# A decoder layer on eight cores: residual adds moved to GpSimd, norm steps spread over the blocks, w_ada pieces moved from the down to the up groups

## The reference

```python
mod = silu(c) @ w_ada + b_ada                       # (B, 6D), D = 2048
shift_m, scale_m, gate_m, shift_f, scale_f, gate_f = split(mod, 6)
h = rms_norm(x, g_pre_mix) * (1 + scale_m) + shift_m
u, v, p, ga, gb = split(h @ w_in)                   # 9216 columns
y_a = spatial_gating(gelu(u), gelu(v), ...) @ w_branch_a
y_b = multiscale_pool(p, ...) @ w_branch_b
mix = (sigmoid(ga) * y_a + sigmoid(gb) * y_b) @ w_out
x = x + gate_m * rms_norm(mix, g_post_mix)
h = rms_norm(x, g_pre_ffn) * (1 + scale_f) + shift_f
up = causal_depthwise_conv(h @ w_up, conv_w, conv_b) # 2 * 5632 columns
a, g = split(up, 2)
x = x + gate_f * rms_norm((gelu(a) * g) @ w_down, g_post_ffn)
```

## Time and profile before

| | us |
|---|---|
| median of 3 runs | 2220.53 |
| lowest, highest | 2217.82, 2484.43 |
| the profiled execution | 2215.26 |
| its span on the slowest core (core 2) | 2213.3 |
| spans of the eight cores | 2198.2 to 2213.3 |
| TensorE matmul busy | 1886.2 (85%) |
| VectorE, ScalarE, GpSimd busy | 714.1, 550.8, 67.2 |

### The profile page before, as it was taken

How to read it: one execution, slowest core, us unless ns; L and a number is a source line. 1 busy time by engine, 2 the same in 40 slices (tenths; PEclk the granted TensorE clock), 3 DMA queues, 4 the chain that set the end, 5 groups by cost and what they waited for, 6 DMA issues and landing times.

```text
span 2213.3 us, 28189 instructions; the slowest of 8 cores (2198.2 to 2213.3 us)
## 1 busy us (share of the span) xinstructions
PE 1886.2 (85%) x12028; PEld 1125.5 (51%) x12028; DVE 714.1 (32%) x832; ACT 550.8 (25%) x722; POOL 67.2 (3%) x113
## 2 busy tenths in 40 slices
PE   0325996999999999999876898799989999899995
PEld 0102443646646565665543564356634665366554
DVE  0114005340111112332556453123532354224535
ACT  0304114100002211113445532024310432034321
POOL 0000000000000000000000000000000000000002
PEclk9857998969999999999998999899999999999998
DMA  9596654642676357555392434553344333443409
GB/s 189 142 168 122 112 93 84 110 81 39 115 133 112 61 96 129 109 106 127 102 175 83 72 72 81 99 101 72 65 91 93 77 67 68 95 85 68 90 16 152
DMA packets 36380, 218.70 MB, mean 99 GB/s; under 512 B 2849, under 2 KB 19489, under 8 KB 24097
## 3 DMA queue, kind: packets, MB, share of 16 engines
q0 software_dynamic: 20192, 187.71, 47.8%
q1 hardware_dynamic: 16066, 29.21, 4.2%
HBM read 379.43 MB, written 16.78 MB: 179 GB/s over the span
## 4 chain that ended last, share of the span: by engine, by line
PE 76%; DMA 7%; DVE 5%; ACT 5%; SPq 3%; issue 3%; DVEq 0%; ACTq 0%; POOLq 0%; POOL 0%
PE ps L289 57%; PE ps L439 6%; PE ps L780 3%; PE ps L1021 3%; PE ps L568 3%; DMA RING<-w_ada 2%; SPq L328 2%; DMA RING<-w_down 2%; SPq L683 1%; DMA RC<-xT 1%; PE ps L494 1%; DMA R<-xT 1%; DMA RING<-w_in 1%; PE ps L488 1%; ACT SC L454 1%
## 5 line engine op out<-in xcount | busy, mean ns | idle before, releaser
L289 PE MATMUL ps<-RD,RING 128*128 128x342 bf16 (+1 forms) x3360 | 578.0, 333 | 73.5 <-DMA RING<-w_down 46.0
L289 PE MATMUL ps<-RC,RING 128*128 128x342 bf16 x3696 | 539.2, 308 | 7.1 <-ACT R L901 7.1
L289 PEld LDWEIGHTS ps<-RD,RING 128*128 128x128 bf16 x3360 | 328.1, 98 | 319.4 <-issue 87.4
L289 PEld LDWEIGHTS ps<-RC,RING 128*128 128x128 bf16 x3696 | 358.6, 97 | 187.6 <-issue 7.4
L842 DVE SCALAR_TENSOR_TENSOR SC<-SC,vec 128x1024 f32<-128x1024 f32 x77 | 98.9, 1285 | 284.7 <-ACT SC L840 284.7
L925 ACT ACTIVATE SC<-ps 128x1026 f32<-128x1026 f32 x77 | 79.0, 1027 | 408.5 <-PE ps L289 399.4
L289 PE MATMUL ps<-R,RING 128*128 128x342 bf16 x1152 | 172.0, 310 | 0.9 <-DVE R L503 0.9
L439 PE MATMUL ps<-RING,RD 128*128 128x512 bf16 x576 | 127.2, 384 | 25.0 <-ACT RD L404 25.0
L289 PEld LDWEIGHTS ps<-R,RING 128*128 128x128 bf16 x1152 | 112.0, 98 | 59.5 <-issue 2.5
L439 PEld LDWEIGHTS ps<-RING,RD 128*128 128x128 bf16 x576 | 56.7, 99 | 94.6 <-issue 28.8
L844 DVE SCALAR_TENSOR_TENSOR SC<-SC,vec 128x1024 f32<-128x1024 f32 x77 | 98.9, 1284 | 8.4 <-DVE SC L842 0.5
(11 more groups left out here) (131 smaller groups left out, 1278.1 us busy)
## 6 DMA issues: line engine op xcount, KB each, us to landing
RING<-w_ada POOLq DMA_DIRECT2D x24, 2048.0 KB, 27.5
RING<-w_in POOLq DMA_DIRECT2D x18, 2048.0 KB, 16.9
RING<-w_up POOLq DMA_DIRECT2D x16, 2048.0 KB, 13.1
RING<-w_down POOLq DMA_DIRECT2D x12, 1408.0 KB, 11.0
RING<-w_up POOLq DMA_DIRECT2D x8, 1536.0 KB, 10.5
R<-xT SPq DMA_DIRECT2D x15, 576.0 KB, 43.6
R<-xT SPq DMA_DIRECT2D x6, 1368.0 KB, 24.3
RING<-w_branch_a POOLq DMA_DIRECT2D x4, 2048.0 KB, 15.8
```

Source lines behind the costliest of these rows:

```text
L289: e.matmul(o, lhsT=l, rhs=r, start=st, stop=sp),
```

## The change

Seven edits:

1. Weight loads get `max_dma_last_dim=4096`: a contiguous run is cut into pieces of at most 4096 bytes of the float32 source (2048 bytes of bf16).
2. The residual parts come from a second input `xP`, laid out on the host so that a partition's 8 channel blocks are one run of 10944 bytes, instead of 8 runs of 1368.
3. The residual add goes from VectorE to GpSimd.
4. The inverse norms of the mix chain lie in PSUM banks 4 and 5, not in SBUF. The mix projection and pass C then take their banks in turn from 0 to 3, pass AB pairs 0/1 and 2/3.
5. The chain of a part is 17 entries of `later` instead of 10: root, invert, 8 pairs, drain, drain and second root, second invert, 4 norms of 4 channel blocks. The ones matmuls follow two pairs later. The last block of a part runs two entries.
6. Mod pieces 20 to 23 move from the down groups behind the first up piece of (group 0, half 1), (1, 0), (1, 1), (2, 0).
7. In the last down group the reciprocal is a queue entry of its own, one entry after an empty one, instead of following the sqrt at once.

```diff
+    xP = din("xP", [3, 128, 16 * 342])
...
-            tok = P.dma("pool", lambda e: e.dma_start(out=flat, in_=src), sem, deps=deps)
+            tok = P.dma("pool", lambda e: e.dma_start(out=flat, in_=src, max_dma_last_dim=4096), sem, deps=deps)
...
-        rstd_m, rstd_x = sc_bufs(12 * 171, PN, 2, F32)
-        tf = sc_bufs(12 * 171 + 2 * PN, PN, 4, F32)
+        tf = sc_bufs(12 * 171, PN, 4, F32)
+
+        rstd_m, rstd_x = bank(4)[:, 0:PN], bank(5)[:, 0:PN]
...
+        def alloc_mid():
+            b = mid_next[0] % 4
+            mid_next[0] += 1
+            return b, bank_free[b]
...
         def load_x(t):
             for q in range(2):
-                P.dma("sp", lambda e, q=q: e.dma_start(out=x_buf[:, q * 8:(q + 1) * 8, :],
-                                                       in_=xT[q * 1024:(q + 1) * 1024, 126 + t * PN:126 + (t + 1) * PN].rearrange("(k p) n -> p k n", p=128)),
+                P.dma("sp", lambda e, q=q: e.dma_start(out=x_buf[:, q * 8:(q + 1) * 8, :].rearrange("p k n -> p (k n)"),
+                                                       in_=xP[t, :, q * 8 * PN:(q + 1) * 8 * PN]),
                       "xp%d" % t, deps=x_free)
...
-        def mix_chain(t, m, t_stat):
-
-            t_s, t_r = inv_rms(rstd_m, bank(6)[:, 0:PN], [t_stat, t_ggm] + rstd_m_free)
-            bank_free[6] = [t_s]
+        def mix_chain(t, m, get_stat):
...
+            def root():
+                state["s"] = P.op("act", lambda e: e.activation(out=rstd_m, in_=bank(6)[:, 0:PN], func=AF.Sqrt, bias=epst[:], scale=1.0),
+                                  deps=[get_stat(), t_ggm] + rstd_m_free)
+                bank_free[6] = [state["s"]]
+
+            def invert():
+                state["r"] = P.op("dve", lambda e: e.reciprocal(out=rstd_m, in_=rstd_m), deps=[state["s"]])
...
             def chunk(b):
                 t_a = P.op("dve", lambda e: e.scalar_tensor_tensor(out=m[:, b, :], in0=m[:, b, :], scalar=ggm[:, b:b + 1], in1=rstd_m,
-                                                                   op0=ALU.mult, op1=ALU.mult), deps=[t_r])
-                t_x = P.op("dve", lambda e: e.tensor_tensor(out=m[:, b, :], in0=m[:, b, :], in1=x_buf[:, b, :], op=ALU.add), deps=[t_a, x_tok[t]])
+                                                                   op0=ALU.mult, op1=ALU.mult), deps=[state["r"]])
+                rstd_m_free[:] = [t_a]
+                t_x = P.op("pool", lambda e: e.tensor_tensor(out=m[:, b, :], in0=m[:, b, :], in1=x_buf[:, b, :], op=ALU.add), deps=[t_a, x_tok[t]])
...
-                return stat2(b, t_sq)
+                pending.append(stat2(b, t_sq))
...
-            def finish():
-                t_s2, t_r2 = inv_rms(rstd_x, bank(7)[:, 0:PN], [state["tok"], t_gsf] + rstd_x_free)
...
             def pair(b):
                 def go():
-                    gos = [chunk(b), chunk(b + 1)]
+                    chunk(b)
+                    chunk(b + 1)
                     if b % 4 == 2:
                         spill_tok[t] = spill(b // 4)
                     if b == KC - 2:
                         x_free[:] = [xm_tok[-1]]
                         if t < 2:
                             load_x(t + 1)
-                    pending.append(gos)
+
+                    while len(pending) > 4:
+                        pending.pop(0)()
                 return go
...
+            def drain():
+                for g in pending[:2]:
+                    g()
+                del pending[:2]
...
+            def invert2():
+                state["r2"] = P.op("dve", lambda e: e.reciprocal(out=rstd_x, in_=rstd_x), deps=[state["s2"]])
+
+            def norm(b0):
                 def go():
...
+                    for b in range(b0, b0 + 4):
...
-            for b in range(0, KC + 2, 2):
-                later.append(step(b))
+            later.extend([root, invert] + [pair(b) for b in range(0, KC, 2)] + [drain, lambda: (drain(), root2()), invert2] + [norm(b) for b in range(0, KC, 4)])
...
-                b, bdeps = alloc_tm()
+                b, bdeps = alloc_mid()
...
-                run_later(1)
+                run_later(2 if blk == KC - 1 else 1)
...
-                def start_chain(t=t, m=m, last_stat=last_stat):
-                    mix_chain(t, m, last_stat())
-                later.append(start_chain)
+                mix_chain(t, m, prev)
...
-            i, bdeps = alloc_blk()
+            b0 = 2 * (m % 2)
+            bdeps = bank_free[b0] + bank_free[b0 + 1]
...
-            bk, bdeps = alloc_tm()
+            bk, bdeps = alloc_mid()
...
                     free_slot(s, tok)
+                    if mod_queue and p == 0:
+                        mod_piece(mod_queue.pop(0))
...
                     free_slot(s, tok)
-                    if mod_queue and (q == 0 or (k == 0 and q == 2)):
-                        mod_piece(mod_queue.pop(0))
...
         def finish_part(j, c0, n, t_stat):
-            t_s, t_r = inv_rms(rstd_y[j][:, 0:n], bank(6 + j % 2)[:, 0:n], [t_stat, t_ggf] + up_done)
+            t_s = P.op("act", lambda e: e.activation(out=rstd_y[j][:, 0:n], in_=bank(6 + j % 2)[:, 0:n], func=AF.Sqrt, bias=epst[:], scale=1.0),
+                       deps=[t_stat, t_ggf] + up_done)
             bank_free[6 + j % 2] = [t_s]
+            t_r = []
+
+            def invert():
+                t_r.append(P.op("dve", lambda e: e.reciprocal(out=rstd_y[j][:, 0:n], in_=rstd_y[j][:, 0:n]), deps=[t_s]))
...
+            fin_q.append(lambda: None)
+            fin_q.append(invert)
...
+        m["xP"] = np.ascontiguousarray(m["xT"][:, 126:].reshape(16, 128, 3, 342).transpose(2, 1, 0, 3).reshape(3, 128, 16 * 342))
```

More of the change, by code:

```diff
@@ L662, in build_program @@
         tf_free = [[] for _ in tf]
-        rstd_m_free = list(gates_done)
-        rstd_x_free = list(gates_done)
+        rstd_m_free = gates_done + bank_free[4]
+        rstd_x_free = gates_done + bank_free[5]
+        mid_next = [0]
+        def alloc_mid():
+            b = mid_next[0] % 4
+            mid_next[0] += 1
+            return b, bank_free[b]
         mix_buf = [part_f32[0], part_f32[2], part_f32[0]]
@@ L743, in go @@
                             load_x(t + 1)
-                    pending.append(gos)
-                return go
-            pending = []
-            def step(b):
-                def go():
-                    if b < KC:
-                        pair(b)()
-                    if len(pending) > (1 if b < KC else 0):
-                        for g in pending.pop(0):
-                            g()
-                    if b >= KC and not pending:
-                        finish()
-                return go
@@ new lines, in invert2 @@
+            def invert2():
+                state["r2"] = P.op("dve", lambda e: e.reciprocal(out=rstd_x, in_=rstd_x), deps=[state["s2"]])
+            def norm(b0):
+                def go():
+                    for b in range(b0, b0 + 4):
+                        f = b % 4
+                        t_a = P.op("dve", lambda e, b=b, f=f: e.scalar_tensor_tensor(out=tf[f], in0=m[:, b, :], scalar=gsf[:, b:b + 1], in1=rstd_x,
+                                                                                     op0=ALU.mult, op1=ALU.mult), deps=[state["r2"]] + tf_free[f])
+                        t_h = P.op("act", lambda e, b=b, f=f: e.activation(out=h2T[:, t, b, :], in_=tf[f], func=AF.Identity,
+                                                                           bias=mod_fm[:, 48 + b:49 + b], scale=1.0), deps=[t_a, mod_tok[15], part_pe[t]])
+                        tf_free[f] = [t_h]
+                        rstd_x_free[:] = [t_a]
+                    if b0 == KC - 4:
+                        if t == 0:
+                            t_h = P.op("dve", lambda e: e.tensor_scalar(out=h2T[:, 0, :, 0:2], in0=h2T[:, 0, :, 0:2], scalar1=hmask[:, 0:1], scalar2=None, op0=ALU.mult),
+                                       deps=[t_h, ldc_all])
+                        h2_tok[t] = t_h
+                        part_free[0 if t != 1 else 2] = [t_a, spill_tok[t]]
+                return go
@@ L805, in build_program @@
             if t < 2:
-                last_stat = prev
-                def start_chain(t=t, m=m, last_stat=last_stat):
-                    mix_chain(t, m, last_stat())
-                later.append(start_chain)
+                mix_chain(t, m, prev)
         mix_dead = tok
-        last_stat = prev
-        def start_chain_c():
-            mix_chain(2, mix_buf[2], last_stat())
-        later.append(start_chain_c)
+        mix_chain(2, mix_buf[2], prev)
         def ffn_up_specs(k, half):
@@ L873, in build_program @@
                     last = kc == KC - 1 and t == 1
-                    tok = P.op("pe", lambda e, i=i, t=t, kc=kc, wt=wt, bl=bl: e.matmul(bank(3 * i + t)[:, 0:PN], lhsT=wt[:, kc, bl * 128:(bl + 1) * 128],
+                    tok = P.op("pe", lambda e, b0=b0, t=t, kc=kc, wt=wt, bl=bl: e.matmul(bank(b0 + t)[:, 0:PN], lhsT=wt[:, kc, bl * 128:(bl + 1) * 128],
```

28 lines of the change are left out of this document (10 added, 18 removed).

## The result

The changed kernel takes 2142.05 us (median of three runs, 2139.89 to 2149.75) against 2220.53: a ratio of 0.966, with a 95% interval of 0.960 to 0.972. The forecast was 2127 us, with a range of its own of 2112 to 2135 and an outer one of 2103 to 2160. The time lies in the outer range and not in the inner. The gain is 78 us where 91 to 93 were expected.

A forecast was written before the change was run, and what follows sets the result against it. TensorE carries 76% of the span and its waits are what an edit can remove; the start is bound by DMA. Gains of 51.2 + 13.5 + 23 + 0 + 3 = 91 us gave 2127, range 2112 to 2135, outer 2103 to 2160.

The forecast's parts named there:

- Down groups: Down groups: without mod pieces the four w_down waits (46.0 us) and half-clock matmuls (4 x 1.3) go, gaining 51.2 us.
- The rest of C to last: Blocks behind pass C: the next needs the eighth L901, the second the eleventh; 1 us gained.
- AB and C: Passes AB and C: ScalarE's queue is the path, 8.9 us per block against 8.74 before; sum 0.
- Start: Kernel start: descriptors of 4096 bytes, queues taking turns one for one, release x at 60, not 73.5; 13.5 us gained.
- the second: Rival: x is not early (grouped packets or slow GpSimd), 9.5 to 13.5 us less gained, 2137 to 2141; chance 0.2.
- Mix blocks: Mix projection: a block takes 2.64 us, a part 42.2; the mix as a whole gains 23 us.
- The wait before AB: End of mix part 2: AB waits 5 us for ScalarE's last norm chunks plus 4 us for w_up.
- Part 0: First part of the mix projection: time as before, with no cost taken for finer load pieces.
- The add on GpSimd: Residual add: 1.0 us taken, between 0.52 and 2.29; in the mix it hides up to 1.3.
- Last group: Last down group: TensorE's waits of 2.94 and 0.96 us behind the reciprocals shrink to about 0.8; 3 us gained.
- multiply and add block each other: Part of rival 3 (chance 0.15): 3.14 us per block, +8 in the mix and +8 in AB, 2143.
- The fifth: Rival: cutting casting loads lowers their rate; at 200 GB/s 2325, deciding from about 225 down; chance 0.05.

The follow-up runs named there:

- e5: The kernel before with one edit only: w_ada (mod) pieces leave the down groups and follow the up pairs; 2170.1 us, ratio 0.9782.
- e2: The changed kernel with the three w_up loads of AB planned as their buffers come free, ahead of later adds on GpSimd's queue; 2138.8 us, ratio 0.9636.
- e4: The changed kernel with the residual add back on VectorE, all else as changed; 2146.7 us, ratio 0.9673.
- e10: The changed kernel with w_up planned early and the next slice's x loaded in two halves; 2143.2 us, ratio 0.9651.
- e8: The kernel before with one edit only: casting loads cut into pieces of 4096 bytes; 2224.3 us, ratio 1.0006.
- second set: The changed kernel unaltered, run again as a base beside the others; 2148.1 us, ratio 0.9662.
- e7: The changed kernel with the inverse norms of the mix stage back in SBUF, not PSUM; 2148.8 us, ratio 0.9668.
- e1: The changed kernel with one part undone: casting loads keep 32-KB descriptors; 2154.8 us, ratio 0.9712.
- e12: The changed kernel with w_up early, x in halves, and AB's mix-chain squares put in ScalarE's wait inside the convolution; 2128.7 us, ratio 0.9586.

## Why the prediction was right or wrong, point by point

The direction and the order of size were right (78 us of 91), the largest term partly by luck. "2124; the median is 5 us over it" gives 2129, and 2127 has no reason for the other 2 us. Two terms were missed by much: the start (10.5 us) and the wait before AB (6 to 9 us). The steps:

- **Down groups** (51.2 us). Right in mechanism: alone it gives 49.0 us on the mean over the cores (e5). The mean wait for w_down was 41.1 us and not core 2's 46.0, which leaves 2.0 us per wait for the half-clock matmuls and not 1.3 (3.0 on core 3). That the two misses nearly cancel is luck. No load in the up groups took its place, but for 3.1 us on core 3 at the first w_up behind C.
- **The rest of C to last** (5.7 us more than in e5, 799.5 against 805.2). This is no gain of its own. The wait of the first block behind pass C for a bank fell from 6.5 to 0.5 us in the mean (the forecast had 1 us here), but C itself starts 3.5 us later behind AB: see AB and C.
- **Start** (13.5 us; 3.0 came). The mechanism, turns of one descriptor for one, was right. Two steps failed. The first is "x costs 128 x 0.416 = 53.3 us, vec and hmask 4, the first issue 3: 60". On core 3 a turn with x took 0.445 us, 57 for the 128; the other 27 turns, of small packets, took 6.5; and they stand behind 5 us: 68.5. The trace doesn't name the transfers of the small packets. The second is "What follows [...] moves with x". In the mean over the cores the last x came 5.0 us earlier (73.2 to 68.2) and gv only 3.0: the waits of TensorE for w_ada between them grew from 32.7 to 34.5 us, since the cut loads are slower. Also the starting point was core 2's 73.5; core 3 had 72.6. Of the rivals this was the second, by its price but not by its mechanism: packets are not grouped. The Trainium skill, DMA: Bandwidth & Descriptors (Queues, rings and completion order), has 9 to 17 descriptors to a packet as typical, with the queue changed only behind a whole packet. The 4-byte packets of this trace, each with a cut piece of the other queue right behind it, don't agree.
- **Mix blocks** (2.64 us, parts of 42.2 and 43.2). Right, a little low: 2.49 us without a pair and 2.79 with one, parts of 43.0 and 44.1.
- **The wait before AB** (5 for the norms and 4 for w_up; 18.0 came). The 5 for the norms is exact: 5.3 us is what stays when w_up is early (e2, e4, e10). The step that failed here is "From there to AB are about 18 us, w_up took 18.9, and x for part 2 comes at the same time: I add 4 us". The sentence names all that went wrong and prices it at 4 where it is 13 on core 3 and 10 in the mean over the cores, so 6 to 9 us of the forecast's gain didn't come: three loads of w_up, x and stores share full DMA engines, and the landing of the first went from 18.9 to 30.5.
- **Part 0** (no change; +2.7 us on core 3, +1.7 in the mean). "The cost of finer pieces: [...] I take none" failed here, at w_out (1.7 and 1.8 us of waits on core 3, none on cores 4 to 7), at w_ada, and at w_down in e8. A cut piece takes 0.216 us and not 0.196.
- **The add on GpSimd** (1.0 us taken; 0.91 measured, bounds 0.52 to 2.29). Right, and that it hides in the mix. What the forecast didn't see is that VectorE would have hidden it there as well (e4), and that GpSimd's queue with the adds in it also decides when w_up goes out.
- **AB and C** (0; -0.7 us). From AB's first matmul to the first behind C the mean went from 113.0 us to 112.3 (111.3 in the second set). The last eviction of AB was forecast 82.9 us behind its start and came at 83.1, and that is partly luck: its periods with two pairs were shorter than 8.9 (8.5) and its first block longer (16.7 for 14.9), from the half clock behind the wait and two late squares. Inside, the border moved: C starts 84.0 us behind AB where it started at 80.0 before (core 3), since the new order of the banks makes its first block wait for AB's last eviction, and the wait at its end is shorter instead. The forecast compared by the first L901, which hid this. The banks were not undone alone.
- **Last group** (3 us; 4.2). TensorE's waits there fell from 4.9 to 1.8 us, the 3 of the forecast. The other 1.1 us and edit 7 itself were not tested.

Of the rivals, "multiply and add block each other" can be seen in e7, and costs 1 us, not 16, since the blocks have room for it. The fifth (loads at a lower rate) happened in small: a tenth, where 225 GB/s would have decided.

What stays open: what each of edits 2, 5 and 7 and the new banks of edit 4 gives by itself, none of them having been undone alone; and whether an order exists in which neither x nor w_up nor the 5.3 us of norm chunks delays AB.

## What to carry to other kernels

When several loads come free at one event (here the last add of a chain releases x's buffer and the GpSimd queue together), price them as one sum of bytes over the engines' rate, not each by its landing alone. Making one early can make the other late: w_up early gained some 10 us before AB and lost 5 in it. And removing a wait gains nothing while another engine's queue is the bound behind it: x in halves took its wait away, and the time stayed. An engine that waits for a neighbour in the middle of its queue (ScalarE 2.16 us for the convolution, then four squares at GpSimd's pace) can take other work into that gap: this reordering gave more (13.3 us) than the choice of engine for the add (5.1 us, and only with w_up issued ahead of it). Test edits in the kernel where they will live: the cut descriptors gave 0 us before and 8 or more after. Read a stage on all cores: on core 3 alone the waits for w_down grew by 8.7 us in e8, in the mean by 4.7, and e1's wait for w_up is not there on the core that was looked at.

## What the runs showed of the hardware

- Casting loads in 4096-byte pieces: 0.216 us per piece and engine, in turns one for one with another queue's packets; issuing one takes GpSimd 0.82 to 0.92 us where 0.53 to 0.57 did with 32-KB runs.
- An add of 128x342 float32 on GpSimd takes 0.91 us, on VectorE 0.52. Beside a VectorE instruction with two SBUF inputs it took 1.11 (the norm multiply, e7) or 1.53 to 1.55 (the convolution's steps, e12), and VectorE's 0.57 became up to 1.22, its 0.93 up to 1.66.
- After a wait for w_down, 22 matmuls of 512 columns took 6.20 us on core 2 (wait of 12.0 us) and 7.77 on core 3 (wait of 9.3), for 4.91: the price of the half clock behind a wait differs by core, and was higher behind the shorter wait.
